# Small matrix products of the matrix-memory stage: before the dense tiles, or between their blocks

## The chip, the cores and the metric

The kernel runs on one core of a Trainium2 chip. The metric is the device time of one execution in microseconds (us): 2462.83 us, the median of three runs (2462.12 to 2464.3). The profile is of one further execution, of 2461.87 us.

## What is computed

One inference step of a decoder with two layers, for 544 token columns: 512 prompt tokens, and 8 sequences of 4 new tokens. Each layer is a half-step SwiGLU feed-forward, a token mixing, a second half-step feed-forward and a gated per-layer embedding, each with RMS norms around it. In the token mixing one dense projection gives z, whose columns go to three groups:

```
z = u @ w_in                                    # 24 tiles of 128 columns
A: windowed softmax attention                   # q, k, v
B: h = RG-LRU scan of conv(xb);  yb = rms(gelu(gb) * h) * g_out_b
C: per chunk of 128 tokens and per head (4 heads of 64):
     Dm = b[t] - b[s] + ig[s], causal;  mt = running max
     A = exp(Dm - mt) * (q @ k^T)
     num = A @ v + wi * (q @ C),  den = sum(A) + wi * (q @ n),  wi = exp(b + m - mt)
     h = num / max(|den|, exp(-mt))
     C, n = wc*C + sum(ws k v), wc*n + sum(ws k)
y = concat(ya, yb, yc) @ w_out
```

The change is in group C (the matrix memory) and in the RMS norm of group B.

## The kernel before

Everything is feature-major: 128 features on the partitions, the 544 tokens along the free axis, in two halves of 272. The dense products are three-pass products of split fp32 (hi and lo parts in fp32r): `block3` issues 6 matmuls of 128x272 for one block of 128 input rows, and `tile` issues 8 such blocks, 48 matmuls, and then signals `used`. A weight chunk (128x1024) comes by DMA into `raw` (two slots), is cast to `wh` by ScalarE (`split`, L1084), and its rest goes to `wl` by VectorE (`weight_lo`, L1479); `wh` and `wl` have four slots (RING), so `split` of chunk G waits until the tile that used chunk G - 4 is done. VectorE takes each finished tile of z from PSUM (`z_tile`, L1677, 128x544) and signals `z_ready`.

The order on each engine is written out by hand. Each engine runs its list in order, so a wait holds up all that stands behind it. The tiles of z are numbered e = 0 to 23; E_TURN is 15, E_ROWS 16, E_MEM 18. In what follows "tile 17" is the dense tile with e = 17. Chunk numbers are counted from the first chunk of z too, so that chunk 21 is the one of tile 21, and chunk 24 is the first of the output projection.

PSUM has 8 banks; T(i) is the pair of banks 2i and 2i+1. From tile 15 on the tiles of z use T(0), tile 16 T(1). Between tiles 15 and 23 TensorE also issues the small products of group C, all plain fp32, each shown in the trace as two passes:

- the row spreads: rows of 4 partitions (one for each head), `dw` and `mt`, spread over 128 partitions by `sel2` (L794): for each row and each pair of heads two matmuls of 4x272, into T(2) or T(3). ScalarE turns them into `wi` and `em` by an exponential (L1260); the `mt` spreads use the same banks, and so wait for these exponentials.
- `spread_g(t)` (L703): the row `gg` of chunk t spread over 128 partitions for each head, into bank 2. ScalarE makes `wt` of it (`spread_exp`, L1219), GpSimd makes it causal.
- `qk(t)` (L715): the q k products of a chunk, into banks 3 and 4. VectorE makes `at` of `wt` and the product, and `kw` (`weigh`, L1818, L1826).
- `read(t)` (L737, L742, L750) and `update(t)` (L760): numerator and denominator of a chunk into bank 5, and the memory's increment into bank 6 or 7. VectorE finishes both (`finish`, `update`).
- `group_mean` (L690) of group B: three products of the squares (128x544 each) with a matrix of ones, into T(0). ScalarE makes the reciprocal root of it in `acc` (`group_rstd`, L1175 and L1176, 128x544 each), VectorE the normed values (`early_normed`, L1664, three of 128x544), ScalarE their hi parts (`early_hi`, L1180) and VectorE their lo parts (`early_lo`, L1670).

TensorE's list from tile 17 on is: tile 17; all four row spreads; `spread_g(0)`; `qk(0)`; and then for t = 0 to 3: `spread_g(t+1)`, tile 18 + t, `qk(t+1)`, `read(t)`, `update(t)`; for t = 1 also the group mean of B and a wait until ScalarE has read it, since the next tile of z overwrites T(0). VectorE does for each t: (for t = 2 the three `early_normed`, for t = 3 the three `early_lo`), then z of tile 18 + t, `weight_lo` of chunk 22 + t, `finish(t)`, `update(t)`, `weigh(t+1)`. ScalarE does `split` of chunk 21, the four exponentials of the row spreads, `spread_exp(0)`, and then for each t `spread_exp(t+1)` and `split` of chunk 22 + t.

SyncE issues the DMAs: the store of the v tiles waits for z of tile 17 (L482), chunks 22 and 23 are behind it; the store of the k tiles waits for z of tile 20 (L485), chunk 24 is behind it.

Of the kernel before, what the change touches and what calls it, by code (L numbers as in the profile page):

```python
# [26 lines left out]
ACT = mybir.ActivationFunctionType  # L27
EXP_LN = "natural_log_exp_and_others"

P = 128  # L30
DEPTH, D, SEQ, NB, NT = 2, 1024, 512, 8, 4
TOK = SEQ + NB * NT
HALF = TOK // 2
# [7 lines left out]
EPS = 1e-6  # L41
# [121 lines left out]
def build(nc, I, O):  # L163
    x_in, weights, par, rgw, consts, pe_in = I["x"], I["weights"], I["par"], I["rgw"], I["consts"], I["pe"]
    ctx = ExitStack()
    with ctx:
# [106 lines left out]
        def T(i):  # L273
            return psum[:, 2 * i:2 * i + 2, 0:HALF]

        x_stat = psum[:, 2:6, HALF:HALF + HALF // 2]
        quarters = lambda v: v.rearrange("p (q n) -> p q n", q=4)

        Y_FF, Y_Z = ([v[:, k] for k in range(KT)] for v in (y_ff, y_z))
        Y_OUT = [xl_y[:, k] for k in range(3)] + [z2[:, k] for k in Y_TILES]  # L280

# [242 lines left out]
        def _(pe):  # L524
# [6 lines left out]
                                        stop=last and n == 2)  # L531
                return ins

            def tile(t, G, between=None):

                pe.wait_ge(lo.sem, G + 1)
                for k in range(KT):
                    if between is not None and k == 4:
                        between()
                    ins = block3(t, G, k, xh[:, k], xl[:, k], k == 0, k == KT - 1)  # L540
                ins.then_inc(used.sem, 1)

# [119 lines left out]
            def mix_tensor(pe, L):  # L662
# [28 lines left out]
                                            stop=(k == len(squares) - 1))  # L691
                    ins.then_inc(gst_done.sem, 1)

                def z_tile(e, t):
                    pe.wait_ge(z_ready.sem, z_ready.at(L, e - 1 if e <= E_ROWS else e))
                    tile(t, G + e)

                def spread_g(t):
                    n = P if t < 4 else 32
                    if t:  # L700
                        pe.wait_ge(we_ready.sem, we_ready.at(L, t))
                    for h in range(HC):
                        ins = pe.matmul(psum[:, 2, h * P:h * P + n], ident[0:HC, h:h + 1].to_broadcast([HC, P]),  # L703
                                        gg[:, t * P:t * P + n], start=True, stop=True)
                    ins.then_inc(gb_done.sem, 1)
# [13 lines left out]
                def read(t):  # L719

                    n = P if t < 4 else 32
                    if t:
                        pe.wait_ge(hc_ready.sem, hc_ready.at(L, t))
                    pe.wait_ge(at_ready.sem, at_ready.at(L, t + 1))
                    if t == 1:
                        pe.wait_ge(qw_ready.sem, qw_ready.at(L, 1))
                    if 1 <= t < 4:
                        pe.wait_ge(cu_ready.sem, cu_ready.at(L, t))
                    if t == 4:
                        pe.wait_ge(sc_loaded.sem, sc_loaded.at(L, 1))  # L730
                    half = [slice(HD * p, HD * p + HD) for p in range(2)]
                    for c in range(2):
                        for den in range(2):
                            o = den * 256 + c * P
                            for p, r in enumerate(half):
                                w = va[0:n, t, 2 * c + p, 0:HD] if not den else con[0:n, K_ONE:K_ONE + HD]
                                ins = pe.matmul(psum[r, 5, o:o + n], w, at_[0:n, 2 * c + p, 0:n],  # L737
                                                start=True, stop=(t == 0))
                            if 1 <= t < 4:
                                for r in half:  # L740
                                    w = cp[r, c, 0:HD] if not den else cp[r, c, HD:HD + 1].to_broadcast([HD, HD])
                                    ins = pe.matmul(psum[r, 5, o:o + n], w, qw[r, c, t * P:t * P + n],  # L742
                                                    start=False, stop=True)
                            if t == 4:
                                for b in range(NB):
                                    for r in half:
                                        w = (cs[r, b, c, 0:HD] if not den
                                             else cs[r, b, c, HD:HD + 1].to_broadcast([HD, HD]))
                                        k = o + NT * b
                                        ins = pe.matmul(psum[r, 5, k:k + NT], w,  # L750
                                                        qw[r, c, SEQ + NT * b:SEQ + NT * b + NT],
                                                        start=False, stop=(b == NB - 1))
                    ins.then_inc(nd_done.sem, 1)
# [28 lines left out]
                    ins = pe.transpose(psum[0:n, 6, t * HC:(t + 1) * HC], gr_[:, t * P:t * P + n], ident[0:HC, 0:HC])  # L782
                ins.then_inc(gc_done.sem, 1)
                z_tile(E_ROWS, 1)
                z_tile(E_ROWS + 1, 0)
                pe.wait_ge(gc_ready.sem, gc_ready.at(L, 1))
                pe.wait_ge(row_ready.sem, row_ready.at(L, 2))
                pe.wait_ge(sel_loaded.sem, sel_loaded.at(L, 1))
                for w, row in enumerate((dw, mt)):
                    for c in range(2):  # L790
                        if w:
                            pe.wait_ge(wb_ready.sem, wb_ready.at(L, c + 1))
                        for h in range(2):
                            ins = pe.matmul(T(2 + c)[:, h, :], sel2[:, c * P:(c + 1) * P],  # L794
                                            row[:, h * HALF:(h + 1) * HALF], start=True, stop=True)
                        ins.then_inc(wb_done.sem, 1)
                pe.wait_ge(z_ready.sem, z_ready.at(L, E_MEM))
                spread_g(0)
                pe.wait_ge(wb_ready.sem, wb_ready.at(L, 4))
                qk(0)  # L800
                for t in range(4):
                    spread_g(t + 1)
                    z_tile(E_MEM + t, 0)
                    qk(t + 1)
                    read(t)
                    update(t)
                    if t == 1:
                        pe.wait_ge(z_ready.sem, z_ready.at(L, E_MEM + 2))
                        group_mean(T(0), ones, [z2[:, k] for k in range(ZXB, ZXB + 3)], 1)
                        pe.wait_ge(gr_ready.sem, gr_ready.at(L, 1))  # L810
                z_tile(E_MEM + 4, 0)
                read(4)
                z_tile(E_MEM + 5, 0)
# [212 lines left out]
            for L in range(DEPTH):  # L1026
# [6 lines left out]
                for e in range(4, E_TURN):  # L1033
                    pe.wait_ge(z_ready.sem, z_ready.at(L, e - 3 if e < 7 else e - 2))
                    n = 2 * e - 15
                    tile((e - 4) % 3, G + X_IN + e, (lambda: recurrent_gate(L, n)) if 8 <= e <= 10 else None)
                    if 7 <= e <= 9:
                        recurrent_gate(L, n + 1)
                mix_tensor(pe, L)
# [35 lines left out]
        def _(act):  # L1075
# [134 lines left out]
            def mix_scalar(L):  # L1210
# [42 lines left out]
                             psum[r, 4 + t % 4, 256:512].rearrange("p (h d) -> p h d", h=HC)).then_inc(tm_ready.sem, 1)  # L1253
                split(G + 15 + RING)
                split(G + 16 + RING)
                split(G + 17 + RING)
                for w, dst in enumerate((wi, em)):
                    for c in range(2):
                        act.wait_ge(wb_done.sem, wb_done.at(L, 2 * w + c + 1))
                        act.activation(dst[:, c, :].rearrange("p (h n) -> p h n", h=2), T(2 + c), ACT.Exp,  # L1260
                                       scale=(1.0, -1.0)[w]).then_inc(wb_ready.sem, 1)
                act.wait_ge(gc_ready.sem, gc_ready.at(L, 1))
                spread_exp(0)
                for t in range(4):
                    spread_exp(t + 1)
                    if t == 2:
                        for n in range(3):
                            early_hi(L, n)
                    split(G + E_MEM + t + RING)
                    if t == 0:  # L1270
                        act.wait_ge(b_done.sem, b_done.at(L, 1))
                        for k in range(3):
                            act.activation(z2[:, ZXB + k], z2[:, ZGB + k], ACT.Square).then_inc(gs_ready.sem, 1)
                    if t == 1:
                        group_rstd(L, 1, acc[:], T(0), DB)
                split(G + E_MEM + 4 + RING)
                act.wait_ge(used.sem, used.at(L, X_OB))
                for n in range(6):
# [193 lines left out]
        def _(ve):  # L1472
# [206 lines left out]
            def mix_vector(L):  # L1679
# [184 lines left out]

                weigh(0)
                for t in range(4):
                    if t == 2:
                        ve.wait_ge(gr_ready.sem, gr_ready.at(L, 1))
                        for n in range(3):
                            early_normed(L, n, acc[:])  # L1870
                    if t == 3:
                        for n in range(3):
                            early_lo(L, n)
                    z_tile(L, E_MEM + t)
                    weight_lo(E + E_MEM + t)
                    finish(t)
                    update(t)
                    weigh(t + 1)
                z_tile(L, E_MEM + 4)
                finish(4)  # L1880
                ve.wait_ge(sc_loaded.sem, sc_loaded.at(L, 1))
# [438 lines left out]
```

## Time and profile before

| | |
|---|---|
| median of 3 runs | 2462.83 us (2462.12 to 2464.3) |
| the profiled execution | 2461.87 us |
| its span, first to last instruction | 2460.2 us |
| TensorE busy with matmuls | 2370.4 us (96%) |
| VectorE busy | 1173.2 us (48%) |
| ScalarE busy | 829.6 us (34%) |
| mean granted TensorE clock | 0.981 |
| DMA, mean | 101 GB/s |

The stretch that the change touches, tiles 17 to 23, lies at about 537 to 624 us in the first layer and at about 1753 to 1841 us in the second. Four views of the profile are used. The chain of waits is the work that ended last, followed back; each line has its start, its length and what it was. The stage windows give for a stretch the busy time of each engine and the granted TensorE clock (1.00 is full speed, 2.4 GHz; 0.50 is 1.2 GHz). The timeline has the instructions of one engine in order, and the DMA view has the issues with their time to landing.

### The profile page before, as it was taken

What the parts mean: (1) busy time and instruction counts of PE and PEld (TensorE: products, weight loads), DVE (VectorE), ACT (ScalarE), POOL (GpSimd) and SP (SyncE); (2) the same over time, 40 slices, a digit from 0 to 9 for tenths busy, and PEclk for the clock granted to TensorE, in tenths of its full rate; (3) what the DMA queues carried; (4) which work ended last, traced back from release to release, by engine and by line L of the source; (5) the groups of instructions that cost most, each with busy time, mean ns of one, the idle gap of its engine ahead of it and who ended that gap; (6) DMA issues with size and microseconds to landing.
All of it is one profiled execution on the core that took longest, in us unless ns stands there. A gap on an engine that the chain in (4) does not pass through costs nothing.

```text
span 2460.2 us, 43100 instructions
## 1 busy us (share of the span) xinstructions
PE 2370.4 (96%) x18938; PEld 2281.8 (93%) x18938; DVE 1173.2 (48%) x1949; ACT 829.6 (34%) x1341; POOL 9.3 (0%) x18
## 2 busy tenths in 40 slices
PE   7999999999899999999999999999998999999997
PEld 7999999998679999999899999999985799999996
DVE  4333334774548333334663333366655573333346
ACT  4222223341345222223552222244315452222243
POOL 0000000000000000000000000000000000000000
PEclk9999999999899999999999999999998999999999
DMA  4322333221652222323222222223217422223321
GB/s 148 92 86 85 96 98 95 79 92 36 226 207 92 89 85 87 102 95 94 80 79 90 85 86 94 95 79 95 75 56 273 173 78 86 87 93 97 100 89 54
DMA packets 74473, 247.54 MB, mean 101 GB/s; under 512 B 14424, under 2 KB 16736, under 8 KB 74336
## 3 DMA queue, kind: packets, MB, share of 16 engines
q1 hardware_dynamic: 74336, 245.59, 30.6%
q8 instruction: 101, 1.65, 0.3%
q14 instruction: 36, 0.29, 0.0%
HBM read 238.68 MB, written 6.88 MB: 100 GB/s over the span
## 4 chain that ended last, share of the span: by engine, by line
PE 90%; DVE 5%; ACT 3%; DMA 1%; issue 1%; SPq 0%; DVEq 0%; ACTq 0%
PE psum L530 72%; PE psum L547 8%; PE psum L835 2%; DMA raw<-in_weights 1%; PE psum L898 1%; DVE wl L1479 1%; PE psum L932 1%; DVE x L1513 1%; ACT wh L1084 1%; PE psum L870 1%; PE psum L703 0%; PE psum L846 0%; PE psum L690 0%; PE psum L658 0%; PE psum L858 0%
## 5 line engine op out<-in xcount | busy, mean ns | idle before, releaser
L1084 ACT CAST wh<-raw 128x1024 fp32r<-128x1024 f32 (+2 forms) x364 | 373.6, 1029 | 1066.4 <-PE psum L530 965.7
L530 PE MATMUL psum<-xh,wh 128*128 128x272 f32 x3472 | 727.7, 291 | 5.3 <-DVE z L1677 3.0
L530 PE MATMUL psum<-xh,wl 128*128 128x272 f32 x3472 | 722.4, 290 | 0.0
L530 PE MATMUL psum<-xl,wh 128*128 128x272 f32 x3472 | 719.9, 289 | 0.0
L1479 DVE TENSOR_TENSOR wl<-raw,wh 128x1024 fp32r<-128x1024 f32 (+2 forms) x364 | 435.8, 1199 | 295.4 <-ACT wh L1084 294.7
L530 PEld LDWEIGHTS psum<-xh,wh 128*128 128x128 f32 x3472 | 550.7, 190 | 9.0 <-DVE z L1677 3.8
L530 PEld LDWEIGHTS psum<-xl,wh 128*128 128x128 f32 x3472 | 549.8, 190 | 0.0
L530 PEld LDWEIGHTS psum<-xh,wl 128*128 128x128 f32 x3472 | 546.1, 190 | 0.0
L530 PE MATMUL psum<-hh,wl 128*128 128x272 f32 x1232 | 255.0, 288 | 0.0
L530 PE MATMUL psum<-hh,wh 128*128 128x272 f32 x1232 | 254.7, 288 | 0.0
L530 PE MATMUL psum<-hl,wh 128*128 128x272 f32 x1232 | 254.0, 288 | 0.0
L1557 DVE TENSOR_TENSOR act_out<-act_out,psum 128x544 f32<-128x544 f32 x84 | 60.6, 721 | 289.5 <-PE psum L530 289.5
L530 PEld LDWEIGHTS psum<-hh,wh 128*128 128x128 f32 x1232 | 193.8, 188 | 0.0
L530 PEld LDWEIGHTS psum<-hl,wh 128*128 128x128 f32 x1232 | 193.6, 189 | 0.0
L530 PEld LDWEIGHTS psum<-hh,wl 128*128 128x128 f32 x1232 | 192.3, 189 | 0.0
L547 PE MATMUL psum<-xh,wh 128*128 128x272 f32 x464 | 140.9, 304 | 28.7 <-DVE xl L2045 11.3
L1542 DVE TENSOR_TENSOR act_out<-psum,r 128x544 f32<-128x544 f32 x84 | 60.8, 724 | 187.7 <-PE psum L530 187.7
L547 PE MATMUL psum<-xh,wl 128*128 128x272 f32 x464 | 136.6, 294 | 0.0
L547 PE MATMUL psum<-xl,wh 128*128 128x272 f32 x464 | 136.3, 294 | 0.0
L547 PEld LDWEIGHTS psum<-xh,wh 128*128 128x128 f32 x464 | 90.1, 194 | 33.6 <-DVE xl L1498 14.1
L1562 DVE TENSOR_TENSOR hl<-act_out,hh 128x544 fp32r<-128x544 f32 x88 | 63.8, 725 | 74.0 <-ACT hh L1133 74.0
L547 PEld LDWEIGHTS psum<-xl,wh 128*128 128x128 f32 x464 | 90.5, 195 | 0.2
(265 smaller groups left out, 2190.2 us busy)
## 6 DMA issues: line engine op xcount, KB each, us to landing
raw<-in_weights SPq DMA_DIRECT2D x340, 512.0 KB, 3.5
kv<-in_kc SPq DMA_DIRECT2D x32, 672.0 KB, 8.2
kv<-in_vc SPq DMA_DIRECT2D x32, 672.0 KB, 6.5
raw<-in_weights SPq DMA_DIRECT2D x16, 320.0 KB, 4.0
raw<-in_weights SPq DMA_DIRECT2D x8, 384.0 KB, 5.3
x<-in_x SPq DMA_DIRECT2D x4, 544.0 KB, 7.5
out_x<-x SPq DMA_DIRECT2D x8, 272.0 KB, 2.1
out_v<-z SPq DMA_DIRECT2D x2, 816.0 KB, 4.3
```

The lines of the kernel that those rows point to most:

```text
L530: ins = pe.matmul(T(t)[:, h, :], w, r[:, h, :], start=first and n == 0, stop=last and n == 2)
L547: ins = pe.matmul(T(t)[:, h, :], w, r[:, h, :], start=first and n == 0, stop=last and n == 2)
L835: ins = pe.matmul(psum[:, bank, 0:HALF], w, r, start=n == 0 and o == 0, stop=n == B_BLOCKS - 1 and o == 2)
L870: ins = pe.matmul(psum[r, 6, 0:P], vt[:, kb, h * HD:(h + 1) * HD], ptp[j % 2][:, p, kb, :], start=(kb == 0), stop=(kb == qb))
L898: ins = pe.matmul(psum[32 * j:32 * j + 32, bank, o:o + k1 - k0], qbd[:, 4 * g + j, c, :], kv[:, half, j, at:at + k1 - k0], start=(c == 0), ...
L932: ins = pe.matmul(psum[rr, 2, lo_ - kb * 384:hi_ - kb * 384], pts[:, kb, rr], kv[:, half, j, lo_ - half * KV_HALF:hi_ - half * KV_HALF], s ...
L1084: act.copy(wh[:, G % RING, 0:n], raw[:, G % 2, 0:n]).then_inc(hi.sem, 1)
L1479: ve.tensor_tensor(wl[:, G % RING, 0:n], raw[:, G % 2, 0:n], wh[:, G % RING, 0:n].bitcast(F32), ALU.subtract).then_inc(lo.sem, 1)
L1513: ve.tensor_tensor(x[:, k, h], x[:, k, h], y[k][:, h], ALU.add).then_inc(xn_ready.sem, 1)
L1542: ve.tensor_tensor(act_out[:, f % 2], T(2 * (f % 2)), r2[:], ALU.mult).then_inc(gate_ready.sem, 1)
L1557: ve.tensor_tensor(act_out[:, b], act_out[:, b], up, ALU.mult).then_inc(h_ready.sem, 1)
L1562: ve.tensor_tensor(hl[:, f], act_out[:, b], hh[:, f].bitcast(F32), ALU.subtract) \
```

## The change

On TensorE the row spreads are no longer one block behind tile 17. `tile` takes a table of things to do ahead of given blocks, and the four spreads (each of two matmuls) stand ahead of blocks 3, 4, 6 and 7 of tile 17. Tile 17 no longer waits for z of tile 16 (it uses the other banks), only for z of tile 15. `qk(0)` goes ahead of block 2 of tile 18, `spread_g(1)` ahead of block 4 of tile 18, and `spread_g(t+1)` for the later t ahead of block 1 of tile 18 + t. The group mean of B goes ahead of block 6 of tile 20, into pieces of banks 5, 6 and 7 in place of T(0) (272, 136 and 136 columns), and `read(2)` waits until ScalarE has read it. ScalarE's `split` of chunk 21 goes behind the exponentials of the row spreads; the reciprocal root goes to t = 2, with the logarithm in three pieces; `early_hi` goes behind the `split` of t = 3. VectorE's `early_normed` and `early_lo` go from ahead of z of tiles 20 and 21 to behind `weigh(3)` and `weigh(4)`.

```diff
+        b_stat = ((psum[:, 5, 0:HALF], slice(0, HALF)),
+                  (psum[:, 6, HALF:HALF + HALF // 2], slice(HALF, HALF + HALF // 2)),
+                  (psum[:, 7, HALF:HALF + HALF // 2], slice(HALF + HALF // 2, TOK)))
-            def tile(t, G, between=None):
+            def tile(t, G, ahead_of={}):
                 pe.wait_ge(lo.sem, G + 1)
                 for k in range(KT):
-                    if between is not None and k == 4:
-                        between()
+                    if k in ahead_of:
+                        ahead_of[k]()
                     ins = block3(t, G, k, xh[:, k], xl[:, k], k == 0, k == KT - 1)
...
+                def group_mean_b():
+                    for k in range(3):
+                        pe.wait_ge(gs_ready.sem, gs_ready.at(L, k + 1))
+                        if k == 0:
+                            pe.wait_ge(cu_ready.sem, cu_ready.at(L, 2))
+                        for dst, cols in b_stat:
+                            ins = pe.matmul(dst, ones, z[:, ZXB + k, cols], start=(k == 0), stop=(k == 2))
+                    ins.then_inc(gst_done.sem, 1)
+                def spread_rows(w, c):
+                    if w == 0 and c == 0:
+                        pe.wait_ge(row_ready.sem, row_ready.at(L, 2))
+                        pe.wait_ge(sel_loaded.sem, sel_loaded.at(L, 1))
+                    if w == 0 and c == 1:
+                        pe.wait_ge(gc_ready.sem, gc_ready.at(L, 1))
+                    if w:
+                        pe.wait_ge(wb_ready.sem, wb_ready.at(L, c + 1))
+                    for h in range(2):
+                        ins = pe.matmul(T(2 + c)[:, h, :], sel2[:, c * P:(c + 1) * P],
+                                        (dw, mt)[w][:, h * HALF:(h + 1) * HALF], start=True, stop=True)
+                    ins.then_inc(wb_done.sem, 1)
+                def z_tile(e, t, ahead_of={}):
+                    pe.wait_ge(z_ready.sem, z_ready.at(L, e - 1 if e <= E_ROWS + 1 else e))
+                    tile(t, G + e, ahead_of)
...
+                    if t == 2:
+                        pe.wait_ge(gr_ready.sem, gr_ready.at(L, 1))
...
-                z_tile(E_ROWS + 1, 0)
...
-                pe.wait_ge(z_ready.sem, z_ready.at(L, E_MEM))
+                z_tile(E_ROWS + 1, 0, {3: lambda: spread_rows(0, 0), 4: lambda: spread_rows(0, 1),
+                                       6: lambda: spread_rows(1, 0), 7: lambda: spread_rows(1, 1)})
+                pe.wait_ge(z_ready.sem, z_ready.at(L, E_ROWS + 1))
                 spread_g(0)
-                pe.wait_ge(wb_ready.sem, wb_ready.at(L, 4))
-                qk(0)
+                def first_qk():
+                    pe.wait_ge(wb_ready.sem, wb_ready.at(L, 4))
+                    qk(0)
                 for t in range(4):
-                    spread_g(t + 1)
-                    z_tile(E_MEM + t, 0)
+                    inside = {4 if t == 0 else 1: lambda: spread_g(t + 1)}
+                    if t == 0:
+                        inside[2] = first_qk
+                    if t == 2:
+                        inside[6] = group_mean_b
+                    z_tile(E_MEM + t, 0, inside)
                     qk(t + 1)
                     read(t)
                     update(t)
-                    if t == 1:
-                        pe.wait_ge(z_ready.sem, z_ready.at(L, E_MEM + 2))
-                        group_mean(T(0), ones, [z2[:, k] for k in range(ZXB, ZXB + 3)], 1)
-                        pe.wait_ge(gr_ready.sem, gr_ready.at(L, 1))
...
-                split(G + 17 + RING)
...
+                split(G + 17 + RING)
...
-                    if t == 1:
-                        group_rstd(L, 1, acc[:], T(0), DB)
+                    if t == 2:
+                        flat = acc[:].rearrange("p h n -> p (h n)")
+                        act.wait_ge(gst_done.sem, gst_done.at(L, 1))
+                        for src, cols in b_stat:
+                            ins = act.activation(flat[:, cols], src, ACT.Ln, bias=EPS, scale=1.0 / DB)
+                        steps.link(ins)
+                        act.activation(acc[:], acc[:], ACT.Exp, scale=-0.5).then_inc(gr_ready.sem, 1)
+                    split(G + E_MEM + t + RING)
+                    if t == 3:
+                        for n in range(3):
+                            early_hi(L, n)
...
                 for t in range(4):
+                    z_tile(L, E_MEM + t)
+                    weight_lo(E + E_MEM + t)
+                    finish(t)
+                    update(t)
+                    weigh(t + 1)
                     if t == 2:
...
                     if t == 3:
...
-                    z_tile(L, E_MEM + t)
-                    weight_lo(E + E_MEM + t)
-                    finish(t)
-                    update(t)
-                    weigh(t + 1)
```

## Rows read from the trace of the kernel before

**Rows 1.** The page: shares of the chain of waits, by engine.

```profile
PE 90%; DVE 5%; ACT 3%; DMA 1%; issue 1%; SPq 0%; DVEq 0%; ACTq 0%
```

**Rows 2.** Chain of waits, first layer, tile 17 to tile 18: start, length, what.

```profile
536.61 0.74 DVE z L1677
537.39 6.29 PE psum L530 x48
543.68 3.97 PE psum L794 x16
547.65 1.72 PE psum L703 x8
...
550.65 2.07 PE psum L703 x8
552.72 8.44 PE psum L530 x48
561.17 0.65 PE psum L715 x8
```

**Rows 3.** The same chain, tile 19, the group mean of B, tile 20.

```profile
563.48 1.08 PE psum L703 x8
564.56 6.22 PE psum L530 x48
...
575.01 2.77 PE psum L690 x12
577.80 0.63 ACT acc L1175
578.46 0.67 ACT acc L1176
579.17 1.15 PE psum L703 x8
580.32 7.76 PE psum L530 x48
```

**Rows 4.** Windows: busy and count of PE, PEld, DVE, ACT, POOL, clock, DMA, GB/s.

```profile
543.60:547.50 3.90, 3.90 (x18) 2.96 (x18) 1.95 (x2) 2.92 (x4) 0.00 (x0) 0.99 0.61 187
...
547.45:557.66 10.21, 10.07 (x47) 9.33 (x46) 2.38 (x4) 2.91 (x9) 1.27 (x2) 0.50 0.31 115
...
581.55:584.96 3.41, 3.41 (x17) 3.41 (x16) 0.09 (x1) 1.58 (x3) 0.64 (x1) 0.50 0.00 0
```

**Rows 5.** Chain of waits, second layer, the places of rows 2 and 3.

```profile
1752.68 0.74 DVE z L1677
...
1777.34 0.65 PE psum L715 x8
...
1791.17 2.77 PE psum L690 x12
...
1804.25 0.74 DVE z L1677
```

**Rows 6.** Chain of waits: fp32 products already inside dense work.

```profile
41.89 0.93 PE psum L564 x8
...
476.90 0.92 PE psum L658 x4
```

**Rows 7.** DMA issues at 544.8 to 545.5 us: count, KB, median us to landing.

```profile
raw<-in_weights SPq DMA_DIRECT2D x1, 512.0 KB, 5.2
```

**Rows 8.** Timeline of VectorE, first layer: the three `early_normed`.

```profile
579.47 2.17 DVE L1664 SCALAR_TENSOR_TENSOR z<-z,pc,acc 128x544 f32<-128x544 f32 x3
```

**Rows 9.** Chain of waits, first layer, behind the end of tile 20.

```profile
588.11 0.73 DVE z L1677
...
589.25 5.15 DMA raw<-in_weights
...
599.95 0.77 DVE at L1818 x2
```

**Rows 10.** Timeline of TensorE, first layer: qk(4), with the idle time before it.

```profile
600.85 0.32 PE L715 MATMUL psum<-z 64*32 64x32 f32 x8 [1.36 <-DVE at L1818]
```

More of the change, by code:

```diff
@@ L692, in group_mean @@
                     ins.then_inc(gst_done.sem, 1)
-                def z_tile(e, t):
-                    pe.wait_ge(z_ready.sem, z_ready.at(L, e - 1 if e <= E_ROWS else e))
-                    tile(t, G + e)
+                def group_mean_b():
[21 more added lines that the diff above has]
+                    tile(t, G + e, ahead_of)
                 def spread_g(t):
@@ L784, in mix_tensor @@
                 z_tile(E_ROWS, 1)
-                z_tile(E_ROWS + 1, 0)
[L786 to L796, printed above, removed]
-                pe.wait_ge(z_ready.sem, z_ready.at(L, E_MEM))
+                z_tile(E_ROWS + 1, 0, {3: lambda: spread_rows(0, 0), 4: lambda: spread_rows(0, 1),
+                                       6: lambda: spread_rows(1, 0), 7: lambda: spread_rows(1, 1)})
+                pe.wait_ge(z_ready.sem, z_ready.at(L, E_ROWS + 1))
                 spread_g(0)
-                pe.wait_ge(wb_ready.sem, wb_ready.at(L, 4))
-                qk(0)
+                def first_qk():
+                    pe.wait_ge(wb_ready.sem, wb_ready.at(L, 4))
+                    qk(0)
                 for t in range(4):
-                    spread_g(t + 1)
-                    z_tile(E_MEM + t, 0)
+                    inside = {4 if t == 0 else 1: lambda: spread_g(t + 1)}
[4 more added lines that the diff above has]
+                    z_tile(E_MEM + t, 0, inside)
                     qk(t + 1)
@@ L1035, in _ @@
                     n = 2 * e - 15
-                    tile((e - 4) % 3, G + X_IN + e, (lambda: recurrent_gate(L, n)) if 8 <= e <= 10 else None)
+                    tile((e - 4) % 3, G + X_IN + e, {4: lambda: recurrent_gate(L, n)} if 8 <= e <= 10 else {})
                     if 7 <= e <= 9:
@@ L1265, in mix_scalar @@
                     spread_exp(t + 1)
[L1266 to L1269, printed above, removed]
                     if t == 0:
```

## The prediction

> **What bounds the kernel.** I read the shares of the chain of waits first: TensorE holds 90% of it [rows 1], so time is won where TensorE waits, where its clock is low, or where it has less to issue. This change issues the same products. So I looked at the chain in the touched stretch for pieces of other engines, and at the stage windows for the granted clock. The reader is to see three things there, in each of the two layers. First, ahead of tile 17 stands VectorE's evacuation of tile 16 (0.74 us; 0.78 from 536.61 to 537.39), though the two tiles lie in different banks [rows 2]. Second, tile 18 takes 8.44 us where tile 19 takes 6.22, and the two g spreads take 1.72 and 2.07 us where the next takes 1.08 [rows 2, 3]. The windows say why: for 3.9 us TensorE issued only products on 4 partitions, at a clock of 0.99 and busy all the time; right behind them the clock was 0.50 for 10.2 us [rows 4]. Third, behind the group mean TensorE waits for ScalarE's logarithm and exponential (0.63 and 0.67 us; 1.39 from 577.78 to 579.17), then comes a g spread, and tile 20 takes 7.76 us [rows 3], with 3.4 us at 0.50 [rows 4].
>
> **Tiles 17 and 18.** Before, from the end of tile 16 to the end of tile 18: 561.17 - 536.61 = 24.56 us in the first layer, 1777.34 - 1752.68 = 24.66 in the second [rows 2, 5]. Afterwards the same products without the wait and at the full clock: tile 17 6.29, row spreads 3.97, g spread 1.08, q k product 0.65, g spread 1.08, tile 18 6.22, which is 19.29 us [rows 2, 3]. That saves 5.27 and 5.37 us; 0.78 of each is the wait, some 4.5 the clock. A switch between the kinds of product within a tile costs nothing that I can see: a recurrent gate product (4 passes of 272 columns) laid inside a tile takes 0.92 us [rows 6], less than 4 of the 16 passes of the row spreads (3.97 / 4 = 0.99). The bounds are 3.68 and 3.97 us for the spreads; I take the upper.
>
> **The group mean.** Before, from its start to the end of tile 20: 588.11 - 575.01 = 13.10 and 1804.25 - 1791.17 = 13.08 us [rows 3, 5]. Afterwards it has 6 passes of 272 columns and 12 of 136: 6 x 2.77 / 12 = 1.39, and 12 x 0.93 / 8 = 1.39 [rows 3, 6], so 2.78 where it was 2.77; the cut costs nothing. With 1.08 for the g spread and 6.22 for the tile that is 10.08 [rows 3]. It saves 3.02 and 3.00 us: 1.39 of waiting, 1.54 of clock and 0.07 in the g spread. The sum at the full clock is 5.27 + 5.37 + 3.02 + 3.00 = 16.7 us.
>
> **What must hide the moves.** Inside a tile a late product holds up all dense blocks behind it, so I follow each new wait. A block takes 6.22 / 8 = 0.78 us.
> - The third and fourth row spreads wait for exponentials (0.62 us each, as the 0.63 of the logarithm on the same size [rows 3]). Between the end of the first spread and the start of the third lie a spread and three blocks, 3.3 us; ScalarE's `split` of chunk 20, ahead of them, starts at tile 17's start and is done before block 3. Spare: over 2 us. Without this cover TensorE would lose the 0.6 us of an exponential at each of the two.
> - `spread_g(1)` waits for the exponentials of `spread_g(0)` (about 1.2 us, and `split` of chunk 21 about 1 us ahead of them); between them lie four blocks and a product, 3.8 us. Uncovered: at most 2.2 us.
> - `read(2)` waits for the reciprocal root: 1.39 us before [rows 3], perhaps 1.6 with the logarithm in three pieces (an estimate: two more starts). Two blocks and a q k product lie over it, 2.2 us. Uncovered: at most 1.6 us. The mean's own wait for `update(1)` is met some 2 us ahead of block 6.
> - `split` of chunk 21 behind the exponentials is at most 1 us later; tile 21 is over 20 us away. The v store and chunk 22 behind it on SyncE wait for z of tile 17. Chunk 22 lands 5.2 us after its issue [rows 7], some 6.5 us after tile 17, and ScalarE wants it at the end of tile 18, 9 us after tile 17. Cover: 2.5 us; before, there were 17.
> - VectorE's `early_normed` (2.17 us [rows 8]) moves to the place where `early_lo` was, so z of tile 21 is read as late as before; `early_lo` goes behind `weigh(4)`, in a time in which VectorE waits for tile 22. Both at nothing.
>
> The wait for `at` ahead of qk(4) stays, although `early_normed` no longer stands ahead of it. It hangs on the chain from z of tile 20 over the k store, the DMA of chunk 24 (5.15 us), its cast and rest, `finish(2)` and `weigh(3)` [rows 9], all counted from the end of tile 20, and TensorE reaches qk(4) with the same products as before: 1.36 us idle, as now [rows 10]. What is saved ahead of tile 20 is kept, since that chain begins at its end.
>
> **The clock afterwards.** This is the open term. The row spreads and the g spread still take 5.0 us (3.97 + 1.08) of the 8.9 from block 3 of tile 17 to the start of tile 18 (five blocks are the other 3.9), now in pieces of 1 us between pieces of 0.8 to 1.6 us of dense blocks. The trace has no such pattern. On the one side: 3.9 us of 4-partition products alone, and the clock fell [rows 4]; 1.39 us idle, 1.15 of g spread and little dense work, and it fell in tile 20 as well [rows 3, 4]. On the other: a g spread of 1.08 us between `update(0)` and tile 19, with tile 19 at 6.22 us, so no fall [rows 3]. The new pattern is nearer to the last but not far from the second. A short fall costs 7.76 - 6.22 = 1.54 us [rows 3]. Bounds: none at all (0), and a low stretch as costly as now (4.5 us for each layer). I take one short fall in one of the two layers: 16.7 - 1.5 = 15.2 us. In tile 20 the mean stands among dense blocks and nothing waits, so I expect no fall there.
>
> Against the profiled execution's own time, 2461.87 us (span 2460.2 and 1.7 around it), that is 2446.7. The median of the runs lies 0.96 above that execution, so I give 2447.6 us.
>
> **A rule that speaks against this.** The row: while the 4-partition products ran, the matmuls were busy for 3.90 of 3.90 us, and the clock fell right after them [rows 4]. The Trainium skill, page "TensorE: Matmul & The Clock Gate", section "What's actually happening", says that the clock is set by how busy the array has been of late. If that is read as the busy time of the profile, the row disagrees, as TensorE had no idle stretch there. By the rule read so, laying busy work among busy work changes nothing in the clock; its result is the second rival below.
>
> **The rivals.**
> - The low clock comes as now in tiles 17 and 18 of both layers, since the small products still take over half of the stretch ahead of tile 18; the waits go and tile 20 is whole. For it: those 5.0 us in 8.9. Against: no 2 us without dense work are left. It gives 2 x 0.78 + 6.0 = 7.6 us, so 2455.2. Chance 0.18.
> - The interleaving does nothing to the clock anywhere, tile 20 too: only the waits go, 2 x (0.78 + 1.39) = 4.3 us, so 2458.5. For it: the clock also fell with TensorE busy. Against: tile 19's g spread. Chance 0.07.
> - The wait ahead of qk(4) also goes, because the k store or chunk 24 gets through faster or `early_normed` did count: 1.36 us in the first layer [rows 10], and I take the same for the second. 15.2 + 2.7 gives 2444.9. Against: the chain of rows 9 has no `early_normed` in it. Chance 0.07.
> - Slower: the clock falls already at the third row spread and stays low up to block 5 of tile 18, because dense work at half the clock, cut by small products, doesn't raise it: the first blocks of tile 18 didn't in the first layer either. Price: 7 blocks at 0.78 more is 5.5, two row spreads at 0.97 more is 1.9, three small products at some 0.6 more is 1.8 [rows 2, 3], 9.2 us for each layer. Tile 20 falls as now. It decides from 4.5 + 0.78 + 1.39 = 6.7 us of loss for each layer on; at 9.2 the kernel is 5.0 us slower, 2467.8. Chance 0.04.
>
> **Numbers.** The forecast case (none to two short falls, 2446.1 to 2449.2) has 0.62; 0.02 is left for no change, as when a wait inside a tile eats the gain. The range goes from 2443.5 (third rival with no fall at all) to 2456.0 (first rival with 0.8 over it); outside are the second rival, the slower one and the rest. A difference below 0.2% (4.9 us) can't be told from none here. Faster: 0.62 + 0.18 + 0.07 = 0.87. Same: 0.07 + 0.02 = 0.09, as 4.3 us is just within. Slower: 0.04.
>
> **What would show it.** Right: tile 17 starts right at tile 16's end; from there to the end of tile 18 about 19.3 us; clock 1.00 there but for one stretch in one layer; from the end of `update(1)` to the end of tile 20 about 10.1 us; no logarithm or exponential of `acc` in the chain; qk(4) still waits 1 to 1.4 us for `at`. Wrong: the clock at 0.50 for 10 us in tiles 17 and 18; a row spread or `spread_g(1)` waiting on ScalarE inside a tile; `read(2)` waiting for `acc`; or no idle time ahead of qk(4).

## The result

The changed kernel takes 2455.22 us, median of 7 runs (2451.4 to 2462.27), against 2462.12 us of the kernel before in the same session (7 runs, 2461.84 to 2464.3): a ratio of 0.9972, 95% interval 0.9962 to 0.9982. It is faster by 6.9 us where 14.5 to 15.2 were forecast. And its runs lie 11 us apart, those of the kernel before 2.5 (in the later sessions, with more runs, it was 6.7 for the changed kernel, and 4.3, 5.9 and 7.3 for the kernel before). The execution that was profiled is its slowest, 2462.27 us (span 2460.5), so a second one of the same kernel is read beside it below (2457.96 us).

The chain of waits of the kernel after, first layer, tile 17 to tile 20; columns as in [rows 2], L534 is a block of a dense tile, L718 the row spreads, L731 the g spreads, L743 q k, L705 the group mean:

```profile
537.40 1.11 PE psum L718 x4
538.51 0.95 PE psum L534 x6
539.47 1.11 PE psum L718 x4
540.57 2.57 PE psum L534 x12
543.15 2.10 PE psum L718 x4
545.25 1.66 PE psum L534 x6
...
550.67 2.00 PE psum L731 x8
552.68 3.02 PE psum L534 x12
...
563.44 0.65 PE psum L743 x8
...
579.09 3.94 PE psum L534 x30
583.03 2.76 PE psum L705 x18
585.80 1.51 PE psum L534 x12
...
588.47 4.96 DMA raw<-in_weights
```

There is no wait ahead of tile 17 and none for the logarithm and exponential of `acc`; tile 20 has its blocks at 0.74 to 0.79 us. That answers to [rows 3] as forecast. But the third row spread takes 2.10 us where the first takes 1.11, and single blocks 1.66. The windows of the kernel after, first and second layer, with the columns of [rows 4]:

```profile
541.10:558.10 17.00, 17.00 (x64) 13.65 (x63) 4.24 (x6) 3.57 (x8) 0.72 (x1) 0.50 0.32 112
558.20:587.20 29.00, 29.00 (x242) 25.75 (x240) 13.40 (x24) 8.49 (x21) 1.90 (x3) 1.00 0.00 1
1766.50:1773.20 6.70, 6.70 (x32) 5.90 (x30) 3.15 (x3) 2.34 (x6) 0.73 (x1) 0.50 0.65 217
1773.30:1803.20 29.90, 29.90 (x250) 26.59 (x248) 14.49 (x27) 8.54 (x21) 1.91 (x3) 1.00 0.04 14
```

The clock was at 0.50 for 17.1 us in the first layer, where it had been there for 10.2 [rows 4], with TensorE busy all the time; in the second for 6.8. (The windows are cut a little inside the low stretches.) From tile 18's later blocks to the end of tile 20 it was at 1.00 in both. And qk(4) waits as before, here 1.16 us [rows 10]:

```profile
599.88 0.32 PE L743 MATMUL psum<-z 64*32 64x32 f32 x8 [1.16 <-DVE at L1846]
```

The stages of all profiles, first and second layer. A tile's end is taken where VectorE starts to read it; "low" is the time at 0.50 within the stage. A profile is one execution: those of e1, e3 and e8 were 1.6 to 3.5 us slower than the medians beside them, and the first one of the changed kernel 7.1.

| kernel | median (range), us | end of 16 to end of 18 | low in it | end of 18 to end of 20 | low in it |
|---|---|---|---|---|---|
| before | 2462.12 (2461.8-2464.3) | 24.6, 24.7 | 10.2, 10.2 | 26.9, 26.9 | 3.4, 3.4 |
| after | 2455.22 (2451.4-2462.3) | 28.3, 23.7 | 17.1, 6.8 | 23.9, 23.9 | 0, 0 |
| after, again | 2458.04 (2456.0-2462.6) | 23.7, 23.7 | 6.8, 6.8 | 23.9, 23.9 | 0, 0 |
| e1, all spreads over 128 rows | 2444.81 (2442.0-2447.3) | 18.5, 18.5 | 0, 0 | 23.1, 23.1 | 0, 0 |
| e2, before + 128 rows | 2451.86 (2449.1-2452.4) | 20.3, 20.3 | 0, 0 | 24.8, 24.8 | 0, 0 |
| e3, row spreads in one block | 2452.28 (2451.3-2455.4) | 22.2, 20.6 | 6.8, 3.4 | 23.9, 23.9 | 0, 0 |
| e4, row spreads alone over 128 | 2448.91 (2446.4-2452.1) | 19.1, 19.1 | 0, 0 | 23.9, 23.9 | 0, 0 |
| e5, one block, 128 rows | 2444.24 (2444.0-2451.3) | 18.4, 18.4 | 0, 0 | 23.1, 23.1 | 0, 0 |
| e6, 4 rows, two blocks apart | 2456.62 (2454.4-2458.1) | 24.7, 23.3 | 6.8, 3.4 | 23.9, 23.9 | 0, 0 |
| e8, before + group mean part | 2458.04 (2455.6-2461.5) | 26.2, 24.6 | 13.7, 10.2 | 23.9, 23.9 | 0, 0 |

The kernel before had its median at 2462.76 us in the session of e0 to e3, at 2462.56 in that of e4 to e7 and at 2464.7 in that of e8. Ratios are to the kernel before of the same session, with their 95% intervals.

### The profile page after: what moved, and what is told of

The parts are those of the page before. It is cut to its first block, busy times and chain, and to the rows that moved or that the text cites. A ratio compares the mean times of both kernels' runs of the same rounds, so it can differ in the third digit from the quotient of the medians.

```text
span 2460.5 us, 43128 instructions
## 1 busy us (share of the span) xinstructions
PE 2375.5 (97%) x18950; PEld 2283.8 (93%) x18950; DVE 1172.9 (48%) x1949; ACT 829.9 (34%) x1345; POOL 9.7 (0%) x18
## 4 chain that ended last, share of the span: by engine, by line
PE 91%; DVE 5%; ACT 3%; DMA 1%; issue 1%; SPq 0%; DVEq 0%; ACTq 0%
PE psum L534 72%; PE psum L551 8%; PE psum L858 2%; DMA raw<-in_weights 1%; PE psum L921 1%; PE psum L955 1%; DVE wl L1507 1%; DVE x L1541 1%; ACT wh L1107 1%; PE psum L893 1%; PE psum L869 0%; PE psum L780 0%; PE psum L662 0%; PE psum L718 0%; PE psum L881 0%
## 5 line engine op out<-in xcount | busy, mean ns | idle before, releaser
L534 PE MATMUL psum<-xh,wh 128*128 128x272 f32 x3472 | 728.9, 291 | 3.6 <-DVE z L1705 1.3
L534 PE MATMUL psum<-xh,wl 128*128 128x272 f32 x3472 | 722.1, 290 | 0.0
L534 PE MATMUL psum<-xl,wh 128*128 128x272 f32 x3472 | 719.4, 289 | 0.0
L534 PEld LDWEIGHTS psum<-xh,wh 128*128 128x128 f32 x3472 | 549.4, 189 | 11.2 <-issue 5.8
L534 PEld LDWEIGHTS psum<-xl,wh 128*128 128x128 f32 x3472 | 549.1, 190 | 0.0
L534 PEld LDWEIGHTS psum<-xh,wl 128*128 128x128 f32 x3472 | 545.9, 190 | 0.0
L534 PE MATMUL psum<-hh,wl 128*128 128x272 f32 x1232 | 255.0, 288 | 0.0
L534 PE MATMUL psum<-hh,wh 128*128 128x272 f32 x1232 | 254.7, 288 | 0.0
L534 PE MATMUL psum<-hl,wh 128*128 128x272 f32 x1232 | 254.0, 288 | 0.0
L534 PEld LDWEIGHTS psum<-hh,wh 128*128 128x128 f32 x1232 | 193.8, 188 | 0.0
L534 PEld LDWEIGHTS psum<-hl,wh 128*128 128x128 f32 x1232 | 193.6, 189 | 0.0
L534 PEld LDWEIGHTS psum<-hh,wl 128*128 128x128 f32 x1232 | 192.3, 189 | 0.0
```

The source lines that it names most:

```text
L534: ins = pe.matmul(T(t)[:, h, :], w, r[:, h, :], start=first and n == 0, stop=last and n == 2)
```

## The experiments

**e0_again: the changed kernel once more.**

> The changed kernel once more. Theory 1 (the clock, not the instruction stream, makes the difference between executions: in tiles 17 and 18 the mixture of 4-partition products and dense blocks lies near the point at which the clock falls): the low stretches there have other lengths than the 17.1 us (first layer) and 6.8 us (second) of the first profile, and the runs scatter over some 10 us, 2451 to 2463, while those of the kernel before stay within 2. Rival (the stream itself has a fixed cost): the same two stretches again, and a profile within 2 us of 2462.

Measured 2458.04 us (11 runs, 2455.97 to 2462.63), ratio 0.9982 (0.9973 to 0.9991). Two windows of its profile:

```profile
547.00:553.80 6.80, 6.80 (x32) 5.93 (x31) 3.15 (x3) 2.38 (x6) 0.72 (x1) 0.50 0.65 219
1762.10:1768.90 6.80, 6.80 (x33) 6.07 (x31) 3.15 (x3) 2.49 (x6) 0.73 (x1) 0.50 0.63 207
```

The same instructions had 17.1 us at 0.50 in the first layer in one execution and 6.8 in another: the stream doesn't fix the loss, as theory 1 has it. That the mixture lies near a point at which the clock falls is not shown by this, and the scatter was less than expected: 6.7 us, against 4.3 of the kernel before. 6.8 us at the low clock make the stage 23.7 us; without them it would be 20.3 (an estimate, half of 6.8 taken off), not the 19.3 of the prediction. All 18 runs of the two sessions have their median at 2457.9.

**e1_full_rows and e2_before_full_rows: the spreads over 128 partitions.** The rows `gg`, `mt` and `dw` lay in the first 4 partitions of a tile that holds finite values in the other 124; the product now reads all 128, with weights that are zero for those (`sel2` is loaded with 128 rows in place of 4).

```diff
-                        ins = pe.matmul(T(2 + c)[:, h, :], sel2[:, c * P:(c + 1) * P],
-                                        (dw, mt)[w][:, h * HALF:(h + 1) * HALF], start=True, stop=True)
+                        ins = pe.matmul(T(2 + c)[:, h, :], sel2[:, c * P:(c + 1) * P],
+                                        (dw_all, mt_all)[w][:, h * HALF:(h + 1) * HALF], start=True, stop=True)
...
-                        ins = pe.matmul(psum[:, 2, h * P:h * P + n], ident[0:HC, h:h + 1].to_broadcast([HC, P]),
-                                        gg[:, t * P:t * P + n], start=True, stop=True)
+                        ins = pe.matmul(psum[:, 2, h * P:h * P + n], ident[:, h:h + 1].to_broadcast([P, P]),
+                                        gg_all[:, t * P:t * P + n], start=True, stop=True)
```

> The changed kernel, with the row spreads and g spreads as products over all 128 partitions (the other 124 rows of the weights are zero), the result the same. Theory 1 (it is the 4 rows that don't count as work for the clock): no stretch at 0.50 between tile 16 and tile 20, 19 to 20 us from the end of tile 16 to the end of tile 18, all runs within 3 us of each other near 2446. It also says whether the 1.11 us of a row spread inside a tile, and the 0.15 more of the block behind it, come from the 4 rows: then 0.92 and none. Rival (small fp32 products between dense blocks lower the clock, whatever their rows): falls as in the changed kernel, 2455 and a wide scatter.

> The kernel before, its order untouched, with row spreads and g spreads over all 128 partitions. Theory 1: the 10.2 us at 0.50 in tile 17/18 go in both layers, worth some 4.5 us each less a wait of 0.6 for the first exponentials that then shows; the fall in tile 20 may go too (1.5 each): 2451 to 2455. Rival (the rows don't matter, the order does): the low stretches stay and the time is 2462.

e1: 2444.81 us, ratio 0.9923 (0.9910 to 0.9937). e2: 2451.86 us, ratio 0.9951 (0.9937 to 0.9964). One window each, from the end of tile 16 to the end of tile 18 in the first layer, e1 and then e2:

```profile
536.50:555.00 18.50, 18.50 (x139) 17.34 (x137) 6.19 (x8) 8.41 (x17) 2.42 (x2) 1.00 0.42 140
```

```profile
535.60:555.90 20.30, 18.84 (x139) 17.51 (x138) 6.28 (x8) 6.77 (x14) 1.27 (x2) 1.00 0.38 127
```

The clock stays at 1.00 in both, also in e2, whose order is that of the kernel before. So it was the products over 4 rows that let the clock fall, and neither the small products as such nor their order. In e2 the fall in tile 20 goes too, though the wait for `acc` is still there: its second stage is 24.8 us, where 26.9 became 23.9 by moving the mean. In the kernel before the row spreads were issued back to back, busy for 3.90 of 3.90 us [rows 4], so it wasn't idle time either. e2's 20.3 us hold 0.73 us for z ahead of tile 17 and a wait for ScalarE's exponentials (L1218) ahead of the second g spread, which the changed order takes away. Its chain of waits:

```profile
535.64 0.73 DVE z L1676
...
542.70 3.81 PE psum L793 x16
546.52 0.91 PE psum L702 x8
...
547.51 1.15 ACT wt L1218 x4
```

The expectation for e2 was met. For e1 the clock and the time came as expected, the stage somewhat shorter (18.5 us, not 19 to 20), and the runs lie 5 us apart, not 3. Its profiled run, 2447.14 us, has 6.8 us at 0.50 behind the wait ahead of qk(4) in the first layer, which e5's, at 2444.03, has not. Between e2 and e1 lies the reordering with the clock held in these stages: 1.8 us (20.3 to 18.5) and 1.7 us (24.8 to 23.1) in each layer, 7.0 us in all, as between their medians.

e1 also shows what a switch between 4-row and 128-row products costs. The chain of waits of e1, first layer (L717 is a row spread, L533 a dense block, L730 a g spread):

```profile
538.75 0.92 PE psum L717 x4
539.67 0.76 PE psum L533 x6
540.43 0.92 PE psum L717 x4
...
546.17 0.89 PE psum L730 x8
```

Over 4 rows the spread is 1.11 us, not 0.92, and the block behind it 0.95, not 0.76. The timeline of the kernel after, second layer, with the weight loads (PEld), says where it lies:

```profile
1757.89 0.75 PEld L718 LDWEIGHTS psum<-dw,sel 4*128 4x128 f32 x4
1757.89 1.18 PE L718 MATMUL psum<-dw,sel 4*128 4x272 f32 x4
1759.00 0.30 PEld L534 LDWEIGHTS psum<-xh,wh 128*128 128x128 f32 x2 [0.36 <-issue]
1759.00 0.52 PE L534 MATMUL psum<-xh,wh 128*128 128x272 f32 x2
```

The weight load of the next dense block starts together with its matmul, after 0.36 us in which no weights were loaded. In dense work a load starts ahead of its matmul. In e1, over 128 rows, the next block's load starts 0.04 us behind the end of the spread's (538.47 + 0.77 = 539.24):

```profile
538.47 0.77 PEld L717 LDWEIGHTS psum<-ge,sel 128*128 128x128 f32 x4
539.28 0.42 PEld L533 LDWEIGHTS psum<-xh,wh 128*128 128x128 f32 x2
```

**e3_rows_block: the row spreads back behind tile 17, all else as changed.**

```diff
-                z_tile(E_ROWS + 1, 0, {3: lambda: spread_rows(0, 0), 4: lambda: spread_rows(0, 1),
-                                       6: lambda: spread_rows(1, 0), 7: lambda: spread_rows(1, 1)})
+                z_tile(E_ROWS + 1, 0)
+                for w in range(2):
+                    for c in range(2):
+                        spread_rows(w, c)
```

> The changed kernel with the four row spreads back in one block behind tile 17; all else as changed. Theory 1: the clock falls behind them for about 10 us in each layer, as before the change, and the gain is that of the waits and of tile 20, 7.6 us: near 2455, with less scatter than the changed kernel; so laying the row spreads between blocks is worth nothing in the median. Rival (the interleaving of the row spreads carries the gain): no better than 2459.

2452.28 us, ratio 0.9956 (0.9942 to 0.9970); its slowest run, 2455.36, is faster than the fastest of the 11 runs of the changed kernel on the same chip, 2455.97. Its chain and its first window:

```profile
541.99 3.92 PE psum L718 x16
545.91 1.34 PE psum L731 x8
547.25 3.02 PE psum L534 x12
```

```profile
546.30:553.00 6.70, 6.70 (x32) 6.00 (x32) 3.52 (x5) 2.25 (x6) 1.78 (x1) 0.50 0.46 159
```

So both were too hard on the block: the clock falls behind it, but for 6.8 and 3.4 us, not 10. Dense work now comes sooner behind it, and that may be the reason; no run tests it alone. Laying the 4-row spreads between the blocks is not worth nothing, it costs 5.8 us against this (2458.04 on the same chip).

**e4_rows_full_only, e5_block_full, e6_apart.** e4 is e1 with the g spreads left on 4 rows. e5 is e3 with the spreads of e1. e6 is the changed kernel with its pieces two blocks apart:

```diff
-                z_tile(E_ROWS + 1, 0, {3: lambda: spread_rows(0, 0), 4: lambda: spread_rows(0, 1),
-                                       6: lambda: spread_rows(1, 0), 7: lambda: spread_rows(1, 1)})
-                pe.wait_ge(z_ready.sem, z_ready.at(L, E_ROWS + 1))
-                spread_g(0)
+                z_tile(E_ROWS + 1, 0, {1: lambda: spread_rows(0, 0), 3: lambda: spread_rows(0, 1),
+                                       5: lambda: spread_rows(1, 0), 7: lambda: spread_rows(1, 1)})
...
-                    inside = {4 if t == 0 else 1: lambda: spread_g(t + 1)}
+                    inside = {5 if t == 0 else 1: lambda: spread_g(t + 1)}
                     if t == 0:
-                        inside[2] = first_qk
+                        inside[1] = lambda: spread_g(0)
+                        inside[3] = first_qk
```

> The changed kernel, with only the row spreads over all 128 partitions; the g spreads stay on 4. If the row spreads are the cause: no low stretch in tiles 17 and 18 or at most a short one, 19 us from the end of tile 16 to the end of tile 18, 2446 to 2448. If the g spreads have a part in it: falls as in the changed kernel, though fewer, 2450 or more.

> The changed kernel with the row spreads in one block behind tile 17 and all spreads over 128 partitions, so that the clock has no part in it. Theory: laying the row spreads between blocks is by itself worth only the wait for the exponentials, 0 to 0.6 us for each layer, so 2445 to 2446 against the 2444.8 of the interleaved one. Rival (the interleaving itself wins time that the clock loss only hid): 2449 or more.

> The changed kernel with its 4-partition spreads two blocks apart: row spreads ahead of blocks 1, 3, 5 and 7 of tile 17, spread_g(0) ahead of block 1 of tile 18, the first q k product ahead of block 3, spread_g(1) ahead of block 5. If the distance between the pieces decides: no fall or one short one in each layer, 20.5 us from the end of tile 16 to the end of tile 18, 2447 to 2450 and little scatter. If 4-partition products among dense work lower the clock however they are laid: 2454 or more.

e4: 2448.91 us (0.9945, 0.9932 to 0.9958). e5: 2444.24 us (0.9929, 0.9917 to 0.9941). e6: 2456.62 us (0.9972, 0.9961 to 0.9982). In e4's profile the clock doesn't fall in tiles 17 to 20, so it is the row spreads. The two stages of each layer are 0.6 and 0.7 us longer than e1's, some 2.6 us in all, for the g spreads over 4 rows; the median lies between the two expectations, 0.9 above the first. Window of e4, from the end of tile 16 to the end of tile 18 in the first layer:

```profile
535.80:554.90 19.10, 19.10 (x139) 17.52 (x137) 6.19 (x8) 8.51 (x17) 2.27 (x2) 1.00 0.40 133
```

In e5 the order of the row spreads changes nothing (18.4 against 18.5 us a layer, where up to 0.6 were expected). In e6 the distance helps little: the clock falls for 6.8 and 3.4 us, the stages would be some 21.4 us without it, not 20.5, and with z of tile 17 now waited for at the start of tile 18 (0.74 us) nothing is won that can be told from the changed kernel (2458.04 on another chip). The time is that of the second expectation, the low stretches are shorter than in the changed kernel:

```profile
547.90:554.50 6.60, 6.60 (x31) 5.71 (x30) 2.11 (x2) 1.14 (x4) 0.64 (x1) 0.50 0.83 286
1766.50:1769.70 3.20, 3.20 (x16) 2.95 (x17) 0.49 (x1) 1.05 (x4) 0.64 (x1) 0.50 0.95 317
```

**e7_before_again and e8_mean_only.** The kernel before for a second profile, and the kernel before with the group mean's part of the change alone (the diff is that part of the change's).

> The kernel before once more, for a second profile of it. Theory: 10.2 us at 0.50 in tiles 17 and 18 of each layer again, or 6.8 at the least, 3.4 in tile 20, and in tile 23 either 3.4 or 6.8 or more, since the low stretches behind the 4-column products of read(4) have other lengths in other executions.

> The kernel before with the group mean's part alone: the mean ahead of block 6 of tile 20, the reciprocal root and the early parts moved with it; row spreads, g spreads, first q k product and the wait ahead of tile 17 as before. If the parts add up: 10.2 us at 0.50 in tiles 17 and 18 as before, none in tile 20, 3.0 us less from the end of tile 18 to the end of tile 20 in each layer, 2456.5. Then the other part of the change (tiles 17 and 18) is worth about zero in the changed kernel, whose 18 runs lie around 2457. If the two parts need each other: 2459 or more.

e7: 2462.08 us; 10.2 us at 0.50 in tiles 17 and 18 in both layers, 3.4 in tile 20, and in tile 23 6.8 and 3.4, where the first profile of the same kernel has 3.4 and 6.8. Windows of e7: tiles 17 and 18, then tile 23 of the first and of the second layer:

```profile
545.60:555.80 10.20, 10.06 (x43) 8.84 (x42) 2.38 (x4) 3.53 (x10) 1.27 (x2) 0.50 0.40 136
...
613.90:620.60 6.70, 6.70 (x61) 6.60 (x60) 3.93 (x9) 0.00 (x0) 0.00 (x0) 0.50 0.00 0
1832.50:1835.80 3.30, 3.30 (x15) 3.30 (x16) 3.16 (x9) 0.00 (x0) 0.00 (x0) 0.50 0.00 0
```

e8: 2458.04 us against 2464.7 of the kernel before in its session, ratio 0.9971 (0.9959 to 0.9983), 6.7 us. The whole change had 6.9 (0.9972), and 4.7 in its second session (0.9982). Window of e8 from the end of tile 18 to that of tile 20:

```profile
561.70:585.50 23.80, 23.80 (x204) 21.00 (x204) 13.37 (x24) 5.78 (x14) 1.27 (x2) 1.00 0.01 1
```

The group mean's part is the gain of the change; the part in tiles 17 and 18 adds nothing that can be measured. By the table it is worth 1.0 us a layer with 6.8 us at 0.50, and loses 3.7 with 17.1. In this profile, e8's slowest run (2461.5 us), the low clock in tiles 17 and 18 of the first layer lasted 13.7 us, longer than the 10 that I expected.

## Why the prediction was wrong

The time lies within the range, but the gain is 6.9 us where 14.5 were forecast; the range reached so far only because it took in the first rival.

- The group mean: right. 26.9 us became 23.9 in each layer, 6.0 us in all as in the working, without a fall in tile 20, and e8 has it alone. The cut into 272, 136 and 136 columns cost nothing (2.76 us).
- The wait ahead of tile 17: right, it is gone.
- The covers: right. No small product in a tile waited more than 0.2 us, and `read(2)` not at all.
- The wait ahead of qk(4): right, it stayed (1.16 us).
- "A switch between the kinds of product within a tile costs nothing": wrong for 4 rows. I took the price from a product over 128 rows [rows 6]; over 4 it is 1.11 + 0.2 us in place of 0.99, so the stage without any fall is 20.3 us, not 19.3. That is 2.0 us for both layers, an estimate (built up from e4's 19.1 us, with 0.19 + 0.19 more for each of the four spreads, the stage is 20.6).
- The clock: this is the step that failed. "I take one short fall in one of the two layers", 1.5 us. In the second profile there are 6.8 us at 0.50 in each layer. 6.8 us at half the clock are 3.4 lost, 6.8 us for both layers, and by the first profile, with 17.1 and 6.8 us, it is 12.0. I had put the pattern nearest to the g spread ahead of tile 19, which didn't lower the clock. That was one 4-row piece of 1.08 us; here it was five in 8.9 us. The rival that had the low clock stay in both layers had 2455.2 and was the nearest to the 2455.22 measured. It was right in its place and its mechanism, not in its length: that was 6.8 us in three of the four stages seen. That the numbers agree is luck: its 9.0 us for the clock stand against 6.8 for the clock and 2.0 for the switches, and the same kernel had its median at 2458.04 in the next session.
- The reading of what was lost before: its sum is right, its split isn't. Between the two g spreads the chain waits 1.28 us, from 549.37 to 550.65, for the exponentials of the first one, while `qk(0)` (0.65 us) runs; the prediction doesn't name this wait. Some 0.6 of the 4.5 us that it gave to the clock in each layer is idle time, so the first rival, in which all waits go, should have had 1.3 us more of gain. And in the second layer the clock fell 2.8 us after the start of the row spreads, at 1762.57, not behind them. Two lines of the chain before:

```profile
549.45 1.15 ACT wt L1219 x4
...
1759.76 4.88 PE psum L794 x16
```

The working's 16.7 less 2.0 less 6.8 is 7.9 us, against 6.9 between the medians; no profile shows a run at the median of 2455.22 or faster. The two that there are gained 3.9 and -0.4 us on the profiled execution before, and most of what lies between them is the 10.2 us more at 0.50 in tiles 17 and 18 (4.6 us of stage). The rest of the difference to 7.9 lies for the most part in a place where the clock falls whatever the change: in tile 23, behind the 4-column products of `read(4)`, the stretches were 3.4 and 6.8 us, and 6.8 and 3.4, in the two profiles of the kernel before, and 6.8 and 10.2, and 10.2 and 10.2, in those of the changed one: 3.4 and 5.1 us more lost. That the changed kernel has the long ones I take for chance, since the profiles of e1 to e8 have 3.4 to 10.2 there too; it is not shown. In e1, e3 and e8 it also fell once behind the wait ahead of qk(4) in the first layer, for 6.8, 3.4 and 6.8 us.

The Trainium skill's rule that the clock follows how busy the array was ("TensorE: Matmul & The Clock Gate", section "What's actually happening"): the runs don't bear it out if busy is the profile's busy time. TensorE was busy for 3.90 of 3.90 us ahead of the fall [rows 4], and in the changed kernel for 17.0 of 17.0 us at 0.50. What decided here was over how many rows it was busy.

## What to carry to other kernels

Here a low clock behind a run of small products wasn't cured by cutting the run apart, so look first at how many rows the products use. If they are spreads or selections over a few partitions, read all 128 with zero weights, if what lies in the other rows is finite: here it took no longer (0.92 us for 1.11, 0.89 for 1.08) and no further place in the memory, and won 10.9 us by itself; with the reordering it was 18 us (2444.8 against 2462.8, 2444.2 against 2462.6), where the reordering alone won 5 to 7. And where the low stretches of a kernel differ from run to run, profile it more than once before its gain is explained.

## What the runs showed of the hardware

- Products over 4 rows back to back or between dense blocks let the clock go to 0.50; the same products over 128 rows, 124 of them with zero weights, kept it at 1.00 in each of the eight stages seen (tiles 17 and 18 of both layers in e1, e2, e4 and e5; in e4 only the row spreads were over 128).
- A product over 4 rows between products over 128 keeps the weight loads from running ahead: 0.36 us without a load behind it, where it was 0.04 with all of them over 128 (e1); the product took 1.11 us for 0.92, the block behind it 0.95 for 0.76.
- The low stretches of one instruction stream differ from execution to execution: 17.1 and 6.8 us in one and the same place.
